# The gates of a gated delta rule: made with tokens on the partitions, and their rows spread by one matmul of high and low halves

## The reference, cut to what matters

```python
beta = jax.nn.sigmoid(b)
g = -jnp.exp(A_log) * jax.nn.softplus(a + dt_bias)        # log decay
# within each chunk of 64 tokens:
G = jnp.cumsum(g, axis=-1)
decay = exp(where(tril, G[:, None] - G[None, :], -inf))
k_beta = k * beta
L = where(strict, (k_beta @ k.T) * decay, 0)
sol = triangular_solve(I + L, [v * beta, k_beta * exp(G)])
q_dec = q * exp(G);  k_dec = k * exp(G_last - G)
# then the recurrence over the 4 chunks of 64 tokens
```

## Time and profile before

| | us |
|---|---|
| runs timed | 1157.34, 1153.98, 1154.15 |
| median of the three | 1154.15 |
| the profiled execution | 1158.51 |
| its span in the trace | 1156.7 |

### The profile page before, as it was taken

One profiled execution on the slowest core, in us unless ns is written; L12 is line 12 of the kernel. 1 busy time (PEld: TensorE's weight loads), 2 busy tenths in 40 slices (PEclk: granted clock), 3 DMA queues, 4 the chain that ended last, 5 costly groups with the idle time before them and its releaser, 6 DMA issues. The chain is left out here.

```text
span 1156.7 us, 23245 instructions
## 1 busy us (share of the span) xinstructions
PE 1137.4 (98%) x10262; PEld 1103.4 (95%) x10262; DVE 768.6 (66%) x875; ACT 603.4 (52%) x692; POOL 206.2 (18%) x129
## 2 busy tenths in 40 slices
PE   8999999999999999999899999999999999999998
PEld 7978899999999999999899999999999999999998
DVE  7999775435456897796768757645666556756453
ACT  6978342242664765565655534433798335544341
POOL 0442353210133200000445400000011002211010
PEclk9999999999999999999999999999999999999999
DMA  8443332333365555655555553445445555556552
GB/s 306 149 142 127 137 111 80 106 110 132 124 222 202 194 185 187 208 190 187 178 178 168 169 187 133 146 146 182 146 146 166 191 190 182 183 187 206 191 187 105
DMA packets 27748, 192.81 MB, mean 167 GB/s; under 512 B 3072, under 2 KB 3200, under 8 KB 4992
## 3 DMA queue, kind: packets, MB, share of 16 engines
q1 hardware_dynamic: 27648, 191.33, 48.9%
HBM read 190.27 MB, written 1.05 MB: 165 GB/s over the span
## 5 line engine op out<-in xcount | busy, mean ns | idle before, releaser
L1225 DVE TENSOR_TENSOR wl<-raw,wh 128x2048 fp32r<-128x2048 f32 (+1 forms) x178 | 421.3, 2369 | 134.9 <-ACT wh L898 134.0
L898 ACT ACTIVATE wh<-raw 128x2048 fp32r<-128x2048 f32 x176 | 336.5, 1913 | 248.3 <-DMA raw<-in_wts 248.0
L563 PE MATMUL psS<-Yh,wh 128*128 128x256 f32 x1056 | 300.3, 284 | 1.4 <-issue 1.1
L563 PE MATMUL psS<-Yl,wh 128*128 128x256 f32 x1056 | 293.4, 278 | 0.0
L563 PE MATMUL psS<-Yh,wl 128*128 128x256 f32 x1056 | 293.4, 278 | 0.0
L563 PE MATMUL psS<-Xh,wh 128*128 128x256 f32 x896 | 260.7, 291 | 4.8 <-issue 3.2
L563 PE MATMUL psS<-Xl,wh 128*128 128x256 f32 x896 | 249.7, 279 | 0.0
L563 PE MATMUL psS<-Xh,wl 128*128 128x256 f32 x896 | 249.7, 279 | 0.0
L563 PEld LDWEIGHTS psS<-Yh,wh 128*128 128x128 f32 x1056 | 199.1, 189 | 4.5 <-issue 3.4
L563 PEld LDWEIGHTS psS<-Yl,wh 128*128 128x128 f32 x1056 | 198.9, 188 | 2.5 <-issue 1.9
L563 PEld LDWEIGHTS psS<-Yh,wl 128*128 128x128 f32 x1056 | 198.4, 188 | 0.0
(11 more groups left out here) (246 smaller groups left out, 2004.6 us busy)
## 6 DMA issues: line engine op xcount, KB each, us to landing
raw<-in_wts SPq DMA_DIRECT2D x176, 1024.0 KB, 4.9
raw<-in_wts SPq DMA_DIRECT2D x2, 512.0 KB, 5.8
gdn<-in_x SPq DMA_DIRECT2D x1, 1024.0 KB, 8.2
out<-head SPq DMA_DIRECT2D x4, 256.0 KB, 2.1
head<-in_x SPq DMA_DIRECT2D x1, 516.0 KB, 4.0
head<-in_x SPq DMA_DIRECT2D x1, 512.0 KB, 5.9
head<-in_sel SPq DMA_DIRECT2D x1, 512.0 KB, 4.8
xf<-in_dr SPq DMA_DIRECT2D x1, 512.0 KB, 5.6
```

Source lines behind the costliest of these rows:

```text
L563: mm = pe.matmul(bank[:, half], a[:, n % SLOTS, p, :], b[:, kk_, :], start=(first and i == 0), stop=(last and i == 2), skip_group_check=True)
L898: act.activation(wh[:, n % SLOTS], raw[:, n % SLOTS], ACT.Copy).then_inc(sem["wh"], 1)
L1225: return dve.tensor_tensor(out, a, b, op)
```

## The change

The gates are computed after a transpose instead of before it. The scaled a and b (64 x 256) go at once through the two transposes of `ab_tok`, now in step 4. All of sigmoid, softplus and the decay is then done on 128 partitions x 16 elements (2 token tiles x 8 heads) in `gw`. The steps are spread anew: `ab_tok` 4, `ab_exp` 5, `ab_den` 6, `ab_ln` 7 (ahead of `l2n` in that step), `ab_decay` 7, `ab_cum` 8. `a_log` and `dt_b` lie as 8 columns on all partitions.

g and beta are each written twice side by side (`gtok`, columns 0 to 7 and 32 to 39), so that the matmuls of `ab_cum` make the rows of G (and now of beta as well) twice, on partitions 0 to 7 and 32 to 39. ACT copies both as `fp32r` to `R` (high half); DVE puts the low half in partitions 32 to 39 of `R`. ACT also copies the selector to `fp32r` (`selr`, 40 x 1024). `rows(h)` multiplies `selr` by `R` over 40 partitions in one `fp32r` matmul for beta and one for G.

```diff
-    put(4, "ab_gates")
-    put(5, "ab_decay")
-    put(7, "ab_tok")
+    put(4, "ab_tok")
+    put(5, "ab_exp")
+    put(6, "ab_den")
+    todo[7].insert([step for step, a in todo[7]].index("l2n"), ("ab_ln", ()))
+    put(7, "ab_decay")
     put(8, "ab_cum")
```

TensorE:

```diff
             def ab_cum():
-                pe.wait_ge(sem["gtok"], 1)
+                pe.wait_ge(sem["gtok"], 2)
...
                 for t in range(2):
-                    mm = pe.matmul(psA[4][0:8, 1, t * P:(t + 1) * P], gtok[:, t, 0:8], tri, start=True, stop=True)
+                    pe.matmul(psA[4][0:40, 1, t * P:(t + 1) * P], gtok[:, 0, t, 0:40], tri, start=True, stop=True)
+                    mm = pe.matmul(psA[5][0:40, 0, t * P:(t + 1) * P], gtok[:, 1, t, 0:40], ident, start=True, stop=True)
...
             def rows(h):
...
-                pe.matmul(psA[4 * (h % 2)][:, 0], sel[32:40, h], G2[32:40, :], start=True, stop=True)
-                pe.matmul(psA[4 * (h % 2) + 1][:, 1], sel[0:8, h], G3, start=True, stop=True).then_inc(sem["row"], 1)
+                pe.matmul(psA[4 * (h % 2)][:, 0], selr[:, h], R[:, 1], start=True, stop=True)
+                pe.matmul(psA[4 * (h % 2) + 1][:, 1], selr[:, h], R[:, 0], start=True, stop=True).then_inc(sem["row"], 1)
```

ScalarE:

```diff
             def ab_cum():
                 exp_ln()
+                act.wait_ge(sem["sel"], 16)
+                act.activation(selr[:], sel[0:40], ACT.Copy).then_inc(sem["selr"], 1)
+                act.wait_ge(sem["gs"], 1)
+                act.activation(R[:, 0], psA[4][0:40, 1], ACT.Copy).then_inc(sem["rh"], 1)
+                act.activation(R[:, 1], psA[5][0:40, 0], ACT.Copy).then_inc(sem["rh"], 1)
                 act.wait_ge(sem["gs"], 3)
```

VectorE:

```diff
             def ab_mm():
                 dve.wait_ge(sem["ab"], 1)
+                tt(abt[:], psA[4][0:64, 0], rb[0:64], ALU.mult, "abv")
+
+            def ab_tok():
+                u, m = gw[:, 0], gw[:, 3]
+                bias = par[:, PAR["dt_b"]:PAR["dt_b"] + 8].unsqueeze(1).broadcast_to([P, 2, H1])
+                dve.wait_ge(sem["abT"], 1)
+                then(2, tt_(u, ab(0), bias, ALU.add))
+                stt(m, u, -1.0, u, ALU.mult, ALU.max, "abv")
+
+            def ab_den():
+                dve.wait_ge(sem["aba"], 3)
+                then(4, dve.tensor_scalar(gw[:, 4:6], gw[:, 1:3], 1.0, None, ALU.add))
+                stt(gw[:, 3], gw[:, 4], -1.0, gw[:, 1], ALU.add, ALU.subtract, "abv")
+
+            def ab_decay():
...
+                dve.wait_ge(sem["aba"], 4)
+                then(6, dve.reciprocal(d, d))
+                then(7, tt_(m, m, d[:, 0], ALU.mult))
+                then(8, tt_(m, gw[:, 1], m, ALU.subtract))
+                then(9, dve.scalar_tensor_tensor(out=m, in0=u, scalar=0.0, in1=m, op0=ALU.max, op1=ALU.add))
+                rate = small[:, 8:16].unsqueeze(1).broadcast_to([P, 2, H1])
+                then(10, dve.scalar_tensor_tensor(out=m, in0=m, scalar=-1.0, in1=rate, op0=ALU.mult, op1=ALU.mult))
                 dve.wait_ge(sem["g2z"], 1)
...
+                dve.tensor_copy(both(0), over(m)).then_inc(sem["gtok"], 1)
+                dve.tensor_copy(both(1), over(d[:, 1])).then_inc(sem["gtok"], 1)
...
             def ab_cum():
                 dve.wait_ge(sem["cum"], 1)
                 dve.tensor_copy(Gs[:], flat(4)[:, 0:64]).then_inc(sem["gs"], 1)
-                dve.tensor_copy(G3, psA[4][0:8, 1]).then_inc(sem["g3"], 1)
...
                 dve.wait_ge(sem["tsa"], 1)
                 tt(TS[:, 2], TS[:, 1], TS[:, 4], ALU.mult, "tb")
+                dve.wait_ge(sem["rh"], 2)
+                tt(R[32:40, 0], psA[4][32:40, 1], f32(R[32:40, 0]), ALU.subtract, "g3")
+                tt(R[32:40, 1], psA[5][32:40, 0], f32(R[32:40, 1]), ALU.subtract, "g3")
```

More of the change, by code:

```diff
@@ L275 @@
 SEMS = """
-ab abT aba aqz abh abl abv abw am ao as at bag bs bst cum cv cx dec dr dt eg ev f1 f1h f2 f2h fp fq2 fs g2 g2z g3
+ab abT aba aqz abh abl abv abw am ao as at bag bs bst cum cv cx dec dr dt eg ev f1 f1h f2 f2h fp fq2 fs g2z g3
 gc gg gs gtok h h0 half hln hsum kb kk kn lt m2 m20 m2h ma mask mc md mm ms ms0 mx mx0 mxh nl nm nsum o oa oah oc
-og ogh on onr or orh out pa_ par pb_ pc pe pn pt qd qk r1 r2 r3 raw0 raw1 raw2 raw3 rawh rb rd res4 rg ri rl ro row rr rs rsp rt rtT
-rtk rtp ry s0 sc sel sg silu sp sq sqh sqp sqr sr ss ss0 ssa st t0 t0c tap tb tk tok tsa uw uwp vn warm wh wh0 wl wl0 xq ws x0 x0h
+og ogh on onr or orh out pa_ par pb_ pc pe pn pt qd qk r1 r2 r3 raw0 raw1 raw2 raw3 rawh rb rd res4 rh rg ri rl ro row rr rs rsp rt rtT
+rtk rtp ry s0 sc sel selr sg silu sp sq sqh sqp sqr sr ss ss0 ssa st t0 t0c tap tb tk tok tsa uw uwp vn warm wh wh0 wl wl0 xq ws x0 x0h
 x1 x1h x2 x3 x3h xT xTb xb xbh xres ya yah zp zs
@@ L304, in program @@
         ss = [sb(f"ss{i}", [P, 2, S]) for i in range(2)]
-        small = sb("small", [P, 64])
+        small = sb("small", [P, 88])
         rtok = sb("rtok", [P, 2])
@@ L322, in program @@
         with ExitStack() as own:
+            sb("under", [P, 6 * KT * S + 4 * S], F32, own)
+            selr = sb("selr", [40, H1, P], F32R, own)
+        with ExitStack() as own:
             Zh, Zl = sb("Zh", [P, KT, S], F32R, own), sb("Zl", [P, KT, S], F32R, own)
@@ L1382, in ab_decay @@
-            def ab_decay():
-                u, m, g = abt[0:8, 1], abt[0:8, 2], G2[0:8]
-                then(7, dve.tensor_tensor(g, g, den[0:8], ALU.mult))
-                then(8, dve.tensor_tensor(g, m, g, ALU.subtract))
-                then(9, dve.scalar_tensor_tensor(out=g, in0=u, scalar=0.0, in1=g, op0=ALU.max, op1=ALU.add))
-                dve.tensor_scalar(g, g, small[0:8, 8:9], -1.0, ALU.mult, ALU.mult).then_inc(sem["g2"], 1)
-            def ab_tok():
-                dve.wait_ge(sem["abT"], 1)
-                dve.tensor_copy(gtok[:], flat(4)[:, 0:80].rearrange("p (t c) -> p t c", t=2)).then_inc(sem["gtok"], 1)
+                tt(abt[:], psA[4][0:64, 0], rb[0:64], ALU.mult, "abv")
@@ new lines, in ab_decay, with both, over @@
+            def ab_decay():
+                u, m, d = gw[:, 0], gw[:, 3], gw[:, 4:6]
+                def both(k):
+                    return gtok[:, k].rearrange("p t (r c) -> p t r c", r=2)[:, :, :, 0:H1]
+                def over(v):
+                    return v.unsqueeze(2).broadcast_to([P, 2, 2, H1])
+                dve.wait_ge(sem["aba"], 4)
[5 more added lines that the diff above has]
+                then(10, dve.scalar_tensor_tensor(out=m, in0=m, scalar=-1.0, in1=rate, op0=ALU.mult, op1=ALU.mult))
+                dve.wait_ge(sem["g2z"], 1)
+                dve.tensor_copy(both(0), over(m)).then_inc(sem["gtok"], 1)
+                dve.tensor_copy(both(1), over(d[:, 1])).then_inc(sem["gtok"], 1)
```

59 lines of the change are left out of this document (24 added, 35 removed).

## The result

The changed kernel takes 1177.11 us in the median of 4 runs (1175.56 to 1178.69); the kernel before, beside it, 1155.74 in 4 (1153.98 to 1160.06). The ratio is 1.0171, with a 95% interval of 1.0138 to 1.0204: some 20 us slower (21.4 between the medians), outside the predicted range and on the other side. The profiled execution took 1178.69 us, with a span of 1176.9.

A forecast was written before the change was run, and what follows sets the result against it. PE was taken as the bound, busy 98%, with DVE and ACT near their limit to 130 us. PE alone would save 8.3 us, but the ACT and DVE chain leaves 3.0: 1154.15 - 3.0 = 1151.2 us, range 1148.6 to 1154.8.

The forecast's parts named there:

- After 160 us PE is the bound again and keeps 3.0 us to the end: Rest of the kernel behind 160 us: PE carries the 3.0 us gained earlier through to the end.
- the rivals: Four other outcomes for the whole kernel: 1145.9 us (7%), 1149.6 (18%), 1152.2 (15%) and 1155.4 (10%).
- D: Steps 5 to 9: VectorE and GpSimd contend and stretch two convolutions by 4.2 us in all, giving 1155.4 us; chance 10%.
- The gap of 2.85 us: PE's wait ahead of stream 8, for DVE to empty block 6's bank, goes: 2.85 us off PE.
- the slow clock of 2.0 us: Stream 8, behind PE's gap: the slow clock goes with the gap, 2.0 us off PE.
- `ab_cum` on PE, +0.5: `ab_cum` gets two more float32 matmuls on PE, costing about 0.5 us in all.
- A pair of `rows` at 0.23: In `rows`, a pair costs 0.23 us instead of 0.73; eight pairs save 4.0 us on PE.
- The taps of block 7 at 73.3: ACT's queue, summed to 19.1 us, ends these taps at 73.3, so step 8's convolution starts about 3.5 us earlier.
- the fixed point: PE's sum for step 5's second `l2n`, starting at 52.80; with 0.3 for transposes, ACT's queue starts at 54.2.
- I take 0.2 each: Eleven small gate instructions in steps 4, 6 and 7 cost 0.2 us each; step 7's seven take 1.4 us.
- the cover: Step 7, ahead of a `take`: 1 us or more of slack from the wait for the taps covers the gate instructions.
- From step 10 to step 14 DVE, ACT and POOL release one another, so the 3.0 us stay 3.0: Steps 10 to 14: with no wait for PE in this chain, step 10's 3.0 us lead is kept whole.

The follow-up runs named there:

- e1: Changed kernel with `small` 56 columns wide instead of 88, putting the operand tiles back at their addresses in the kernel before; 1161.55 us, ratio 1.0019.
- e2: Kernel before with `small` 96 columns wide instead of 64, moving the operand tiles 128 bytes on, no instruction changed; 1173.35 us, ratio 1.0127.
- e9: e1's kernel with VectorE's `ab_decay` ahead of the split of block 10 in block 7; 1159.72 us, ratio 1.0022.
- e12: e9's kernel with ScalarE's copy of the selector rows moved from block 8 to the end of block 3; 1159.02 us, ratio 1.0007.
- e5: e1's kernel with the step `ab_cum` one block later, 9 in place of 8, on every engine; 1163.0 us, ratio 1.0047.
- e8: Changed kernel with `small` 120 columns wide, operand tiles 256 bytes behind their place in the kernel before; 1163.78 us, timed once.
- e3: Changed kernel with `small` 64 columns wide, operand tiles 32 bytes further on than in the kernel before; 1182.06 us, ratio 1.0213.
- e13: e12's kernel with `small` 48 columns wide, operand tiles 32 bytes before their place in the kernel before; 1176.74 us, ratio 1.0154.
- e14: e12's kernel with `small` 32 columns wide, operand tiles 96 bytes before their place in the kernel before; 1189.77 us, timed once.
- e15: e12's kernel with `small` 80 columns wide, operand tiles 96 bytes behind their place in the kernel before; 1170.63 us, timed once.
- e7: Changed kernel with `small` 40 columns wide, operand tiles 64 bytes before their place in the kernel before; 1185.85 us, timed once.
- e4: Changed kernel with `small` 72 columns wide, operand tiles 64 bytes further on than in the kernel before; 1192.91 us, ratio 1.0303.

## Why the prediction was wrong

The step that failed is the last one of the sum, "After 160 us PE is the bound again and keeps 3.0 us to the end". PE was the bound, but the sum counted only instructions that the change touches, and put a change of PE's pace at nothing without a reason. The pace went from 115.07 to 117.64 ns from stream 0 on, 21.8 us, because `par` and `small` grew. e1 and e2 show this from both sides. None of the rivals had it either; D (1155.4) alone pointed to slower, by a mechanism that costs 2.1 us in e9; that it lay on the right side is luck.

Point by point, with the place put aside:

- The gap of 2.85 us and the slow clock of 2.0 us ahead of and in stream 8: right. By e1's stream starts, the time from stream 7 to stream 8 is 3.23 us shorter and stream 8 itself 2.38; two parts that together were forecast at 4.85 came to 5.6.
- `ab_cum` on PE, +0.5: right, 0.55 in e9, where nothing waits in stream 9.
- A pair of `rows` at 0.23: wrong, 0.51 in the changed kernel. The step "two `fp32r` matmuls of 256 columns at 0.113 each" left out that starts around them are 0.2 apart and not 0.11. It was of no consequence, since PE is not the bound there.
- The taps of block 7 at 73.3, for the convolution of step 8 at 73.4: in e1 they end at 74.38, 1.1 us later. ACT's queue was added up well: 19.1 us from its start to these taps, as forecast. What failed is the fixed point. PE's sum for the second `l2n` of step 5 starts at 53.87, 1.1 us later than before where 0.3 was allowed for, and ACT takes it up at 55.29 in place of 54.2. And DVE was not free by then: in the changed kernel the convolution started at 76.17, behind the gates and `take`.
- The failed step of the local sum is "I take 0.2 each" for the small gate instructions. The seven of step 7 took 3.94 us, not 1.4. Alone they do cost 0.17 to 0.35; beside POOL about 1. The upper bound of 1.25 that I had from the rows is what they reach there. I had named the contention for convolutions (rival D), and not for the instructions that PE would wait for.
- The consequence that I drew from it was wrong too: I looked for the cover in front of `take`, but it was PE that ran out of it, at `ab_cum`, which waits for `gtok`. That wait of 2.65 us, and the slow clock behind it, pushed the column sums of stream 10, ACT's chain behind them, and with them the convolution of step 10 to 94.38, where 88.6 was forecast and 91.63 was the time before; and that of step 14 to 129.37, for 123.6.
- "From step 10 to step 14 DVE, ACT and POOL release one another, so the 3.0 us stay 3.0": right as a mechanism. The shift of step 10's convolution is the shift of stream 17 in e1 (2.38 and 2.37), in e9 (0.28 and 0.28) and in e12 (-1.19 and -1.18). It does not hold in e5 (1.52 and 2.31), where `ab_cum` lies behind it and PE waits again at `rows`.
- Rival D's reading holds: the convolution and the split of step 9 lose 2.1 us to POOL in e9. The Trainium skill (SBUF — State Buffer, Who interferes with whom), which I cited for it, fits the products of 16 elements too: the length of the instruction doesn't matter, it waits for POOL's. In the changed kernel the three slow ones end at 72.93, 74.15 and 75.15, each 0.03 to 0.04 us behind an instruction of POOL.

So the change itself, at an equal place, costs 2.4 us at stream 17 as it was built (e1), and gains 1.2 us with two mends (e12); the forecast was a gain of 3.0.

What stays open: why the pace depends on the distance of the tiles, and why at some distances it changes between streams, from 113.3 to 117.8 ns and back in the kernel before. The switches are not in the same streams in each execution: streams 41 to 48 ran at 113.3 in the kernel before and at 117.8 in e1, at the same addresses of these tiles. At +128 the two levels are the same two (e2); what differs from the place of the kernel before is the number of streams at 113.3. That all of the run-to-run spread comes from this was not tested.

## What to carry to other kernels

Before pricing a change in a kernel that PE bounds, compare where the tiles lie before and after: a few more columns of a small tile can move every operand, and here 128 bytes cost more than all of the intended effects together. Hold the place fixed (pad, or size the small tiles) when judging the change, and read the pace from the count of matmuls in a pure stretch. And where several engines release one another, follow the one instruction whose shift comes out at the end (here DVE's convolution of step 10); an idle gap of PE that is removed upstream of it is not a gain yet.

## What the runs showed of the hardware

- Matmuls of 128 x 128 by 256 columns in `fp32r`, all at a granted clock of 1.00, start every 113.3, 116.7, 117.3, 117.8, 118.3, 118.7 or 120.0 ns, depending on the distance in bytes from the stationary tiles to the moving tiles. 256 bytes more gave the same again (e8, one run), and exchanging the roles of the two tiles exchanges the paces of a distance and its negative (e3, e13, e14, e15).
- At some distances the pace also changes between streams of one execution: 113.3 and 117.8 ns in the kernel before and in e2 (+128), 117.3, 118.7 and 120.0 in e13 (-32), 118.7 and 120.0 in e7 (-64). At others it stays: 118.3 in e3 and 120.0 in e4 in all streams of the first FFN. The time is restless with it: the kernel before ran from 1153.24 to 1165.43 us on one chip (13 runs), e2 from 1167.38 to 1174.78, but e3 only from 1181.13 to 1183.77 and e4 from 1192.19 to 1194.54 (four runs each).
- A VectorE instruction of 16 elements costs 0.17 us alone and about 1 us beside a GpSimd product of 128 x 512. So does one with a single input: the copy of `gtok` took 1.25 us in e9, where POOL started 0.08 us ahead of it. Not every one does: the reciprocal on 32 elements took 0.34 us beside POOL in the changed kernel and 0.35 alone in e9.
